# Delta rule of an RWKV-7 layer: products of k and v moved to the off-diagonal quarters of TensorE

## The chip, the cores and the metric

The kernel runs on one core of one Trainium2 chip. Its time is the device time of one launch in microseconds (us), the median of several runs. PE is TensorE, PEld its weight loads, DVE VectorE, ACT ScalarE, POOL GpSimd, SP the engine that issues the DMAs.

## The reference, cut to what matters

The whole kernel is one inference step of a two-layer decoder: an RWKV-7 layer, then a sliding-window attention layer, for a prompt of 1024 tokens and eight samples of 8 tokens. The change touches only the recurrence of the first layer. For each of 16 heads of 64 channels:

```
def step(S, inp):
    r_t, w_t, k_t, v_t, kk_t, b_t = inp
    sa = einsum('bhvk,bhk->bhv', S, kk_t)
    S = S * w_t[:, :, None, :] - sa[..., None] * b_t[:, :, None, :] + v_t[..., None] * k_t[:, :, None, :]
    return S, einsum('bhvk,bhk->bhv', S, r_t)
S_fin, ys = lax.scan(step, wkv0, seq)
```

followed by a norm of each head's output, a bonus term from r, k and v, and a multiplication by a gate. All of it is float32.

## The kernel before, in words

The stages follow one another on the core: `mixed_projections` (the projections of the first layer), `delta_rule` (the recurrence), an output projection with layer norm, the projections of the attention layer, the attention, and a last output projection. `delta_rule` begins near 491 us of the profiled span and ends near 861 us.

`delta_rule` replaces the scan by chunks of 64 tokens: 16 chunks of the prompt (`SAMPLE` is 16) and a 17th, which holds all samples. Heads stand in pairs: channels 0 to 63 of the 128 partitions are one head, 64 to 127 the other, and `DT` = 8 pairs make the 16 heads. Every product of a head is 64 by 64 (or 64 by 32, 64 by 128), with operands in one half of the partitions and its result in the same half of a PSUM bank. `HALVES` are the two halves; `for p in HALVES` issues a product of the first head and one of the second. In the 128x128 array of TensorE the first stands in the upper left quarter, the second in the lower right one. The profile writes such a product as `64*64`. Each float32 product gives two records of matmul and two of weight load.

For a chunk c these steps follow one another:

- `make_grams` (L1056): all products of b and k with kk and r over the chunk's tokens; half k = 0 of `bk` is b, k = 1 is k. `mask_grams` on DVE (L1373) cuts them to the lower triangle into `grams`. Index 0 and 1 are products of b, 2 and 3 of k.
- Inversion of the triangular matrix of index 0: POOL takes its 8x8 diagonal blocks (`small`), DVE sums them (`sum_blocks`), POOL spreads them (`pick`), PE spreads them again over the partitions (`spread_blocks`, L1089), DVE solves them by 14 small dependent instructions (`solve_blocks`, L1389), and then three levels of doubling follow: PE `make_lm` (L1097), ACT `keep_lm`, PE `grow` (L1108), DVE `add_grown` (L1413).
- `turn_rows` (L1075): b and k turned and scaled, ACT `keep_rows` into `rows`.
- `make_z` (L1119): state times kk plus grams 2 times v. `make_u` (L1139): inverse times z. `make_s` (L1148): rows of b times u plus rows of k times v. `make_y` (L1157): state times r, grams 1 times u, grams 3 times v.
- Norm, bonus and gate of y on DVE, ACT and POOL, with a transpose on PE in between (`turn_y`, L1175). DVE `gate_y` (L1464) is its end.

The order of the work is written by hand: each engine has one loop `for i in TURNS` (PE from L1218, ACT L1334, DVE L1478, POOL L1003, SP L930). In turn i chunk i + 1 is `front` (grams, rows, blocks), chunk i is inverted and gets its z, and chunk i - 1 is `behind` (u, s, y, norm). On PE a turn is: turn_y(i - 2), spread_blocks(i), make_u(behind), two quarters of the grams, make_s, make_y, the other two quarters of the grams among the levels of the inversion, turn_rows, make_z(i), the last level. Semaphores count how far each step is; an engine waits in its own order, and everything behind a waiting instruction waits too. SP issues per turn b and k, kk and r, v, the gate, and the store of y.

Two PSUM banks hold grams and then the turned rows, one z, u and s (`chain_bank`), one y (`wide_bank`), two the left factors of the inversion, two the grown parts.

Of the kernel before, what the change touches and what calls it, by code (L numbers as in the profile page):

```python
# [763 lines left out]

def first_of_delta(nc, group, a, scr):
# [20 lines left out]
    def load(sp):  # L786
# [7 lines left out]
        sp.dma_start(d["v_rows"][:, 0], scr["vt"][0]).then_inc(d["v_loaded"][0], 16)  # L794
# [8 lines left out]
def delta_rule(nc, group, a, scr, keep, outp, first, g_stored, s_stored, ahead):  # L803
# [6 lines left out]
    with Tensors(nc, "delta", group) as m:  # L810
# [22 lines left out]
        own_turned = m.sb("own_turned", 128, DT, 2, 64)  # L833
        gram_mask, level_mask, same_block, block_mask, row_pick, unit8, block_ones, ident, unit64, gn_g, gn_b, seq_mask = (
# [8 lines left out]
        consts_loaded, kr_loaded, bk_loaded, v_loaded = (first[x] for x in ("consts_loaded", "kr_loaded", "bk_loaded", "v_loaded"))  # L843
        zeroed, gate_loaded = m.sem("zeroed"), [m.sem(f"gate_loaded{k}") for k in range(2)]
        y_stored, s_loaded, kr_own_loaded = [m.sem(f"y_stored{k}") for k in range(2)], first["s_loaded"], first["kr_own_loaded"]
        state_stored = m.sem("state_stored")
        gram_made, gram_kept, small_made, coeff_made, picked, spread = (m.sem(x) for x in (
            "gram_made", "gram_kept", "small_made", "coeff_made", "picked", "spread"))
# [3 lines left out]
        end_spread, rows_made, rows_kept = m.sem("end_spread"), m.sem("rows_made"), m.sem("rows_kept")  # L852
        z_made, z_kept, u_made, u_kept, s_made, s_kept, s_ended = (m.sem(x) for x in (
            "z_made", "z_kept", "u_made", "u_kept", "s_made", "s_kept", "s_ended"))
        bonus_made, y_made, normed, y_squared, y_rooted, y_turned, y_gated = (m.sem(x) for x in (
# [5 lines left out]
        HALVES = (slice(0, 64), slice(64, 128))  # L861
        SAMPLE = 2 * TILES
# [35 lines left out]
        with nc.Block() as block:  # L898
            @block.sync
            def _(sp):  # L900
                def load_operands(c):
                    t, cols = place(c)
                    if c >= 2:
                        sp.wait_ge(rows_made, 2 * (c - 1))
# [5 lines left out]
                def load_values(c):  # L910
                    if c >= 3:
                        sp.wait_ge(y_made, c - 2)
                        sp.wait_ge(bonus_made, 2 * (c - 2))
                    sp.dma_start(v_rows[:, c % 3], scr["vt"][c]).then_inc(v_loaded[c % 3], 16)
# [15 lines left out]
                for i in range(SAMPLE + 3):  # L930
# [6 lines left out]
                    if live(i):  # L937
                        load_gate(i)
                    if i == SAMPLE + 1:

# [19 lines left out]
            def _(pool):  # L960
# [5 lines left out]
                def spread_end(c):  # L966

                    if c:
                        pool.wait_ge(rows_made, 2 * c)
# [3 lines left out]
                def scale_sample():  # L973
                    pool.wait_ge(bk_loaded[SAMPLE % 2], 16 * (SAMPLE // 2 + 1))
                    pool.wait_ge(rows_made, 2 * SAMPLE)
# [5 lines left out]
                def add_bonus(c):  # L981
                    pool.wait_ge(v_loaded[c % 3], 16 * (c // 3 + 1))
# [3 lines left out]
                    pool.tensor_tensor(bonus[:], v_rows[:, c % 3], per_head(keep["bonus"][:, c, :]), ALU.mult).then_inc(bonus_made, 1)  # L986
# [14 lines left out]

                for i in TURNS:
# [5 lines left out]
                    if 0 <= behind < SAMPLE:  # L1008
                        end_state(behind)
                    if live(behind):  # L1010
                        add_bonus(behind)
                    if live(behind) and not live(front):
                        scale_gain(behind)
                    if live(front):
                        lower = grams[:, front % 3, :, 0, :]
                        pool.wait_ge(gram_kept, 4 * front + 4)
                        if 0 <= i < SAMPLE:

                            pool.wait_ge(inv_turned, TURNED * i + 4)
                        if front:  # L1020
                            pool.wait_ge(coeff_made, front)
                        pool.tensor_tensor(small[:], lower, over_heads(same_block[:]), ALU.mult).then_inc(small_made, 1)
                        if live(behind):
                            scale_gain(behind)
                        pool.wait_ge(coeff_made, front + 1)
                        if front:
                            pool.wait_ge(spread, front)
# [1652 lines left out]
```

## Time and profile before

| | us |
|---|---|
| median of three runs | 1472.77 |
| lowest and highest run | 1472.65, 1475.62 |
| span of the profiled execution | 1471.6 |
| PE busy in it | 1411.4 (96%) |
| DVE busy in it | 794.4 (54%) |
| ACT busy in it | 575.6 (39%) |
| POOL busy in it | 249.8 (17%) |

The profiled execution is one of its own. Its page gives the span alone; the runs' times also hold what lies around it, and their lowest is 1.05 us above the span. Busy shares are over the whole kernel; the stage of the change has its own, shown further down. A row of the timeline gives the start, the length, the engine and line, output and inputs, the shape and the number of merged records; in brackets is the idle time of the engine before it and what ended it. Matmuls overlap, so the time that a group costs is read from its start to the next group's start.

### The profile page before, as it was taken

The page shows a single profiled execution, that of the slowest core. Times are in us where ns is not written, and L with a number is a line of the kernel's source. Part 1 is how long each engine was busy: PE and PEld are TensorE (multiplying, and loading weights), DVE is VectorE, ACT ScalarE, POOL GpSimd, SP SyncE. Part 2 cuts the span into 40 slices and gives each one's busy share as a digit, 9 for nine tenths or more (in the row PEclk, how much of TensorE's full clock was granted, in tenths as well). Part 3 has the DMA queues.
Part 4 walks back from the last instruction along what each step waited for, and adds up shares of the span by engine and source line. Part 5 has one row for each costly group of instructions (what it writes and reads, how often), then busy time and mean ns, then how long its engine had stood idle before and what let it go on. Part 6 is the DMA issues. An engine that isn't in the chain of part 4 may idle for free. (4 is left out here: it accounts for less than half of the span.)

```text
span 1471.6 us, 37545 instructions
## 1 busy us (share of the span) xinstructions
PE 1411.4 (96%) x16154; PEld 1281.0 (87%) x16154; DVE 794.4 (54%) x1588; ACT 575.6 (39%) x1178; POOL 249.8 (17%) x351
## 2 busy tenths in 40 slices
PE   7999999999999899999999979999999999998997
PEld 7989899887899899999999858899999997665885
DVE  6737345777831377777777753651112122775545
ACT  6726246777832022222122232441111132886324
POOL 0000000000000256555554700000001000214000
PEclk9999999999999999999999999999999998999999
DMA  5723222567596244335534255024234236431202
GB/s 207 225 60 89 74 89 90 143 188 233 167 256 179 75 97 100 74 87 118 118 88 105 68 196 186 29 111 130 88 90 119 73 108 184 137 105 33 88 29 94
DMA packets 246358, 174.00 MB, mean 118 GB/s; under 512 B 150799, under 2 KB 220367, under 8 KB 245279
## 3 DMA queue, kind: packets, MB, share of 16 engines
q1 hardware_dynamic: 214231, 156.64, 36.9%
q10 hardware_dynamic: 31968, 15.04, 3.6%
q8 instruction: 123, 2.02, 0.6%
q14 instruction: 36, 0.29, 0.1%
HBM read 111.49 MB, written 60.46 MB: 117 GB/s over the span
## 5 line engine op out<-in xcount | busy, mean ns | idle before, releaser
L369 PE MATMUL mix_acc<-mix_high,mix_w_high 128*128 128x364 f32 (+1 forms) x768 | 178.2, 341 | 11.2 <-ACT mix_high L435 9.9
L369 PE MATMUL mix_acc<-mix_low,mix_w_high 128*128 128x364 f32 (+1 forms) x768 | 172.1, 333 | 0.6 <-DVE mix_low L589 0.6
L369 PE MATMUL mix_acc<-mix_high,mix_w_low 128*128 128x364 f32 (+1 forms) x768 | 171.1, 331 | 0.0
L369 PEld LDWEIGHTS mix_acc<-mix_high,mix_w_high 128*128 128x128 f32 x768 | 130.4, 190 | 30.1 <-issue 28.3
L369 PEld LDWEIGHTS mix_acc<-mix_low,mix_w_high 128*128 128x128 f32 x768 | 133.4, 190 | 1.2 <-DVE mix_low L589 0.9
L369 PEld LDWEIGHTS mix_acc<-mix_high,mix_w_low 128*128 128x128 f32 x768 | 133.9, 190 | 0.0
L1528 PE MATMUL out_acc<-qkvg_room_r_high,qkvg_room_w_high 128*128 128x364 f32 (+1 forms) x320 | 105.8, 331 | 2.2 <-DVE qkvg_room_w_low L1880 2.2
L603 DVE TENSOR_TENSOR mix_w_low<-mix_wt,mix_w_high 128x1024 fp32r<-128x1024 f32 x32 | 39.2, 1224 | 126.1 <-ACT mix_w_high L441 125.8
L1528 PE MATMUL out_acc<-qkvg_room_r_low,qkvg_room_w_high 128*128 128x364 f32 (+1 forms) x320 | 105.1, 329 | 0.0
L1528 PE MATMUL out_acc<-qkvg_room_r_high,qkvg_room_w_low 128*128 128x364 f32 (+1 forms) x320 | 105.1, 329 | 0.0
L1878 DVE CAST qkvg_room_w_high<-qkvg_room_wt 128x1024 fp32r<-128x1024 f32 x20 | 14.0, 699 | 156.9 <-DMA qkvg_room_wt<-in_w_att 156.9
L1311 ACT ACTIVATE delta_lm<-delta_lm 128x128 f32<-128x128 f32 x96 | 24.7, 272 | 186.3 <-PE delta_lm L1105 186.3
L455 ACT ACTIVATE mix_out<-mix_acc 128x364 f32<-128x364 f32 (+1 forms) x96 | 38.3, 472 | 146.4 <-PE mix_acc L369 146.3
L1070 PE MATMUL delta_gram<-delta_kr,delta_bk 64*64 64x128 f32 x1088 | 70.8, 273 | 5.2 <-PEq L60 2.3
L584 DVE SCALAR_TENSOR_TENSOR early_xs<-early_xpad,mix_rest_mu,early_xs 128x1024 f32<-128x1024 f32 x96 | 68.7, 780 | 6.7 <-ACT early_xs L419 6.5
L288 POOL MEMSET mix_decay<- 128x16 f32 x8 | 1.0, 129 | 404.0 <-ACT mix_decay L509 404.0
L1925 ACT ACTIVATE qkvg_room_out<-out_acc 128x364 f32<-128x364 f32 (+1 forms) x40 | 18.7, 474 | 123.2 <-PE out_acc L1528 122.0
L1380 DVE TENSOR_TENSOR delta_grams<-delta_gram,delta_gram_mask 128x512 f32<-128x512 f32 x68 | 44.8, 677 | 40.8 <-PE delta_gram L1070 40.6
L1070 PEld LDWEIGHTS delta_gram<-delta_kr,delta_bk 64*64 64x64 f32 x1088 | 60.4, 135 | 6.3 <-issue 4.7
L1528 PEld LDWEIGHTS out_acc<-qkvg_room_r_high,qkvg_room_w_high 128*128 128x128 f32 x320 | 60.2, 188 | 2.5 <-issue 2.5
L2367 ACT ACTIVATE att_score<-att_score,att_low 128x256 f32<-128x256 f32 (+1 forms) x128 | 61.5, 488 | 1.5 <-DVE att_low L2404 1.5
L1713 ACT ACTIVATE begun_work<-all_x 128x1024 f32<-128x1024 f32 x18 | 19.1, 1061 | 108.4 <-DVE all_x L1778 108.4
(280 smaller groups left out, 3412.6 us busy)
## 6 DMA issues: line engine op xcount, KB each, us to landing
mix_wt<-in_w_in SPq DMA_DIRECT2D x32, 512.0 KB, 4.6
qkvg_room_wt<-in_w_att SPq DMA_DIRECT2D x20, 512.0 KB, 3.8
delta_bk<-scr_bk SPq DMA_DIRECT2D x17, 512.0 KB, 4.7
delta_kr<-scr_kr SPq DMA_DIRECT2D x17, 512.0 KB, 7.2
scr_kr<-mix_outs SPq DMA_DIRECT2D x16, 512.0 KB, 3.9
scr_bk<-mix_outs SPq DMA_DIRECT2D x16, 512.0 KB, 4.6
early_xpad<-in_xpad SPq DMA_DIRECT2D x8, 548.5 KB, 8.5
scr_xg<-early_xs SPq DMA_DIRECT2D x8, 544.0 KB, 3.0
```

The costliest lines, as they stand in the source:

```text
L369: mm = pe.matmul(acc[:, s, k, 0:width], w[:, s, d, :], r[:, d, n0:n0 + width], start=d == 0 and q == 0, stop=d == DT - 1 and q == 2)
L455: act.activation(out[:, s, n0:n0 + width], acc[:, s, k, 0:width], ACT.Silu if n >= G_ * DT else ACT.Copy).then_inc(evacuated, 1)
L584: dve.scalar_tensor_tensor(o[k], x[k], rest_mu[:, place, d:d + 1], o[k], ALU.mult, ALU.add).then_inc(mixed, 1)
L603: dve.tensor_tensor(w_low[:, n % 2], wt[:, n % 2], w_high[:, n % 2].bitcast(F32), ALU.subtract).then_inc(w_split, 1)
L1070: mm = pe.matmul(gram_bank[n % 2][p, 256 * j + 128 * k:256 * j + 128 * k + 128], bk[p, c % 2, k, pair, :], kr[p, c % 4, :, pair, :], start ...
L1311: act.activation(blocks(lm[:, lev, 4 * g:4 * g + 4, :].rearrange("p j n -> p (j n)"), lev, 0), lm_bank[g][:, 0:128].rearrange("p (m b) -> ...
L1380: dve.tensor_tensor(grams[:, c % 3, 2 * n:2 * n + 2], gram_bank[n % 2][:, :].rearrange("p (j k n) -> p j k n", j=2, k=4), mask, ALU.mult). ...
L1528: mm = pe.matmul(out, w[:, d, :], r[:, d, columns], start=d == 0 and k == 0, stop=d == DT - 1 and k == 2)
L1713: act.activation(work[:, 1], x[:, t, :], ACT.Copy, accum_out=sums[:, t:t + 1]).then_inc(summed, 1)
L1878: dve.tensor_copy(w_high[:, s], wt[:, s]).then_inc(w_rounded, 1)
L1925: act.activation(out[:, s, n0:n0 + n], banks[s][k][:, 0:n], ACT.Silu if name == "ag" else ACT.Copy).then_inc(evacuated, 1)
L2367: act.activation(score[:, t % 2, h, 0:width(t)], score[:, t % 2, h, 0:width(t)], ACT.Exp, bias=low[:, h:h + 1], accum_out=sums[:, t % 2, h ...
```

## The change

1. v is loaded with its two halves swapped (two DMAs of half the size; `v_rows`), so that the first head's v stands in partitions 64 to 127. A second, unswapped copy (`v_plain`, one more DMA of 256 KB per chunk) serves the bonus on POOL. The products of k in `make_grams` and `turn_rows` write to the other half than they read. So all products of k and v stand in the lower left or upper right quarter, those of b, u, the state and the inversion in the other two.
2. The order on PE puts each off-diagonal product beside a diagonal one of another bank: k beside b in the grams and the rows, grams 2 times v beside the last `make_lm`, grams 3 times v beside `make_u`, rows of k times v beside the end of y.
3. The grams come in two halves of four pairs instead of four quarters of two; each half fills both banks. DVE masks them in four instructions as before, of another cut.
4. `turn_y` and `gate_y` of `behind` stand at the end of a turn, not at the start of the next; `spread_blocks(front)` and the first four of seven columns of the solving too. ACT sets up the solving and POOL scales the state earlier. The mask of the third level of the inversion is dropped: `make_lm` reads `grams` there.

```
+    for half in (slice(0, 64), slice(64, 128)):
+        sp.dma_start(d["v_rows"][half, 0], scr["vt"][0, other_half(half)])...
+    FLIPPED = HALVES[::-1]
...
     def load_values(c):
         if c >= 3:
             sp.wait_ge(y_made, c - 2)
-            sp.wait_ge(bonus_made, 2 * (c - 2))
-        sp.dma_start(v_rows[:, c % 3], scr["vt"][c]).then_inc(v_loaded[c % 3], 16)
+            sp.wait_ge(s_made, c - 2)
+        for p, f in zip(HALVES, FLIPPED):
+            sp.dma_start(v_rows[f, c % 3], scr["vt"][c, p]).then_inc(v_loaded[c % 3], 16)
+    def load_plain_values(c): ...   # after load_gate(c), into v_plain
...
-    def make_grams(c, n):
+    def make_grams(c, h):
+        for j in range(4):
+            pair = 4 * h + j
+            for p in HALVES:
+                first = pe.matmul(gram_bank[0][p, 128 * j:128 * j + 128], bk[p, c % 2, 0, pair, :], kr[p, c % 4, :, pair, :], ...)
+            for p, f in zip(HALVES, FLIPPED):
+                second = pe.matmul(gram_bank[1][f, 128 * j:128 * j + 128], bk[p, c % 2, 1, pair, :], kr[p, c % 4, :, pair, :], ...)
...
+    def turn_rows(c):
+        for pair in range(DT):
+            for k, sides in enumerate((HALVES, FLIPPED)):
+                for p, f in zip(HALVES, sides):
+                    unit = end_diag[p, pair, :] if c < SAMPLE else unit64[p, :]
+                    mm = pe.matmul(gram_bank[k][f, 64 * pair:64 * pair + 64], bk[p, slot, k, pair, :], unit, ...)
...
+    def value_product(c, pair, bank, stands, begun):
+        for p, f in zip(HALVES, FLIPPED):
+            mm = pe.matmul(bank[p, 64 * pair:64 * pair + 64], stands[f], v_rows[f, c % 3, pair, :], start=pair == 0, stop=False, ...)
+        if pair == DT - 1:
+            mm.then_inc(begun, 1)
...
     # make_lm(i, 2): after each pair begin_z(i, pair) = value_product(.. chain_bank, grams 2)
     # make_u(behind): after each pair value_product(.. wide_bank, grams 3)
+    def state_of_y(c): ...          # state times r, 16 products
+    def end_y(c): ...               # grams 1 times u, after each pair value_product(.. chain_bank, rows of k)
+    def end_s(c): ...               # rows of b times u, 16 products
...
 PE, turn i:
+    make_u(behind); make_grams(front, 0); state_of_y(behind); end_y(behind)
+    make_lm(i, 0); end_s(behind); grow(i, 0); make_grams(front, 1)
+    make_lm(i, 1); grow(i, 1); turn_rows(front)
+    make_lm(i, 2, with begin_z); grow(i, 2); end_z(i)
+    turn_y(behind); spread_blocks(front)
 ACT, turn i:
+    keep_z, keep_u(behind); keep_lm(i, 0); square_y(behind); keep_lm(i, 1); begin_solving(front)
+    root(behind); keep_rows(front, 1); keep_rows(front, 0); keep_lm(i, 2)
 DVE, turn i:
+    solve_columns(i, range(4, 7)); widen_blocks(i); mask_grams(front, 0, 0); mask_grams(front, 0, 1)
+    centre_y(behind); add_grown(i, 0); mask_grams(front, 1, 0); add_state(behind); sum_squares(behind)
+    mask_grams(front, 1, 1); invert_root(behind); add_grown(i, 1); sum_blocks(front); scale_y(behind)
+    add_grown(i, 2); gate_y(behind); solve_columns(front, range(4))
 POOL, turn i:
+    spread_end(front); add_bonus(behind); sum_diagonal(front); end_state(i); scale_gain(behind)
+    pick_rows(front); mask_level(front, 0); mask_level(front, 1)
```

## Rows read from the trace of the kernel before

**Rows 1.** The page, span and its first part: busy us, share, instructions.
```profile
span 1471.6 us, 37545 instructions
PE 1411.4 (96%) x16154; PEld 1281.0 (87%) x16154; DVE 794.4 (54%) x1588; ACT 575.6 (39%) x1178; POOL 249.8 (17%) x351
```

**Rows 2.** Busy by stretch: PE, PEld, DVE, ACT, POOL, PEclk, DMA share, GB/s.
```profile
521.65:830.32 308.67, 301.34 (x8764) 296.93 (x8761) 234.15 (x585) 69.80 (x197) 181.83 (x176) 1.00 0.42 96
830.32:844.87 14.55, 13.28 (x311) 9.92 (x309) 9.09 (x23) 3.55 (x7) 11.12 (x11) 1.00 0.48 130
```

**Rows 3.** Timeline of PE over one turn of the delta rule.
```profile
642.26 0.66 PE L1182 MATMUL delta_gram<-delta_ident,delta_y 128*128 128x128 f32 x4
642.75 0.72 PE L1094 MATMUL delta_lm<-delta_pick,delta_block_ones 128*128 128x224 f32 x4
643.40 1.15 PE L1145 MATMUL delta_chain<-delta_z,delta_inv 64*64 64x64 f32 x32
644.38 1.92 PE L1070 MATMUL delta_gram<-delta_kr,delta_bk 64*64 64x128 f32 x32
646.13 0.28 PE L1154 MATMUL delta_chain<-delta_u,delta_rows 64*64 64x64 f32 x4
...
648.00 0.28 PE L1166 MATMUL delta_wide<-delta_state,delta_kr 64*64 64x64 f32 x4
...
650.80 1.04 PE L1070 MATMUL delta_gram<-delta_kr,delta_bk 64*64 64x128 f32 x16
651.67 1.07 PE L1105 MATMUL delta_lm<-delta_inv,delta_below 64*64 64x32 f32 x32
652.58 1.07 PE L1070 MATMUL delta_gram<-delta_kr,delta_bk 64*64 64x128 f32 x16
...
654.38 1.13 PE L1085 MATMUL delta_gram<-delta_end_diag,delta_bk 64*64 64x64 f32 x32
655.34 1.08 PE L1105 MATMUL delta_lm<-delta_inv,delta_below 64*64 64x32 f32 x32
...
657.78 0.31 PE L1131 MATMUL delta_chain<-delta_state,delta_kr 64*64 64x64 f32 x4
...
659.68 1.07 PE L1105 MATMUL delta_lm<-delta_inv,delta_below 64*64 64x32 f32 x32
...
662.08 0.65 PE L1182 MATMUL delta_gram<-delta_ident,delta_y 128*128 128x128 f32 x4
```

**Rows 4.** Timelines of single instants: diagonal quarters, then the attention's column and row halves.
```profile
842.07 0.27 PE L1145 MATMUL delta_chain<-delta_z,delta_inv 64*64 64x64 f32 x2 [0.56 <-ACT delta_z L1298]
...
1281.54 0.14 PEld L2330 LDWEIGHTS att_pv<-att_prob_t,att_v_rows 128*64 128x64 f32 x2 [0.33 <-issue]
...
1281.81 0.60 PE L2330 MATMUL att_pv<-att_prob_t,att_v_rows 128*64 128x256 f32 x4
...
1282.03 0.39 PE L2330 MATMUL att_pv<-att_prob_t,att_v_rows 128*64 128x256 f32 x2
...
1280.48 0.49 PE L2314 MATMUL att_sc<-att_keys,att_q_in 64*128 64x256 f32 x2
```

**Rows 5.** Timeline of DVE over the same turn.
```profile
643.56 0.21 DVE L1397 TENSOR_TENSOR delta_lm<-delta_solved,delta_lm 128x56 f32<-128x56 f32 x1
...
646.72 1.27 DVE L1407 TENSOR_TENSOR delta_inv<-delta_solved,delta_block_mask 128x512 f32<-128x512 f32 x1
...
648.73 1.25 DVE L1380 TENSOR_TENSOR delta_grams<-delta_gram,delta_gram_mask 128x512 f32<-128x512 f32 x2
...
658.61 1.04 DVE L1387 TENSOR_REDUCE delta_coeff<-delta_small 128x64 f32<-128x512 f32 x1
...
661.73 0.29 DVE L1418 TENSOR_TENSOR delta_inv<-delta_inv,delta_grown 128x128 f32<-128x128 f32 x1 [0.75 <-PE delta_grown L1115]
```

**Rows 6.** Timeline of ACT, the second copy of the turned rows.
```profile
661.29 0.60 ACT L1318 ACTIVATE delta_rows<-delta_gram 128x512 f32<-128x512 f32 x1 [0.22 <-PE delta_gram L1085]
```

**Rows 7.** What PE waited for in 520 to 845 us: total, times, longest.
```profile
PE delta_lm L1105 <- issue: 2.1, 2, 1.1
```

More of the change, by code:

```diff
@@ L762, in store_tiles, with other_half @@
     eng.dma_start(dram[TILES, :, j, 0:NB * NT], row[:, SEQ:N]).then_inc(stored, 16)
+def other_half(half):
+    return slice(64 - half.start, 128 - half.start)
 def first_of_delta(nc, group, a, scr):
@@ L1145, in make_u, with state_of_y @@
                             mm = pe.matmul(chain_bank[p, 64 * pair:64 * pair + 64], inverse(c, 1)[p, pair, :], z[p, pair, :], start=True, stop=True)
-                    mm.then_inc(u_made, 1)
-                def make_s(c):
+                        if pair == DT - 1:
+                            mm.then_inc(u_made, 1)
+                        value_product(c, pair, wide_bank, grams[:, c % 3, pair, 3, :], y_begun)
+                def state_of_y(c):
+                    pe.wait_ge(y_begun, c + 1)
+                    for pair in range(DT):
+                        for p in HALVES:
+                            o = wide_bank[p, 64 * pair:64 * pair + 64]
+                            if c < SAMPLE:
+                                pe.matmul(o, kr[p, c % 4, 1, pair, :], state[p, c % 2, pair, :], start=False, stop=False, skip_group_check=True)
+                            else:
+                                pe.matmul(o, own_turned[p, pair, 1, :], unit64[p, :], start=False, stop=False, skip_group_check=True)
@@ L1149, in make_s, with end_y @@
+                def end_y(c):
                     pe.wait_ge(u_kept, c + 1)
[L1150 removed]
+                    if c < SAMPLE:
+                        pe.wait_ge(rows_kept[1], c + 1)
                     for pair in range(DT):
[L1152 to L1154 removed]
@@ L1279, in _ @@
                     if 0 <= i < SAMPLE:
+                        wait_for_z(i)
+                        make_lm(i, 2, lambda pair: begin_z(i, pair))
                         grow(i, 2)
+                        end_z(i)
+                    if i == SAMPLE:
+                        own_values((0,))
+                        wait_for_z(i)
+                        for pair in range(DT):
+                            begin_z(i, pair)
+                        own_values((1,))
+                        end_z(i)
+                    if 0 <= behind < SAMPLE:
+                        turn_y(behind)
+                    if live(front):
+                        spread_blocks(front)
+                    if behind == SAMPLE:
+                        own_updates(range(4))
+                        own_values((4,))
+                        for pair in range(4, DT):
+                            if pair + 1 < DT:
+                                own_values((pair + 1,))
+                            own_updates((pair,))
+                        turn_y(SAMPLE)
             @block.scalar
@@ L1392, in solve_blocks @@
                     term = lm_bank[0][:, 0:64].rearrange("p (u n) -> p u n", u=8)
-                    for j in range(7):
+                    for j in columns:
                         row0 = 0 if j < 4 else 4
@@ L1521, in _ @@
                         add_grown(i, 2)
+                    if 0 <= behind < SAMPLE:
+                        gate_y(behind)
+                    if live(front):
+                        solve_columns(front, range(4))
 def three_passes(pe, out, w_high, w_low, r_high, r_low, columns):
```

309 lines of the change are left out of this document (145 added, 164 removed).

## The prediction

> **What bounds the kernel now.** I read the page first: TensorE is busy 96% of the span, DVE 54% [rows 1]. That is a mean over six stages, so I next cut out the stage that the change touches. In its 15 full turns, 521.65 to 830.32 us, PE is busy 301.3 of 308.7 us, DVE 234, POOL 182, ACT 70, and the clock is granted in full [rows 2]. Then the timeline of PE over one turn. The reader should see there that no row has a bracket with idle time: a turn takes 19.82 us, from one turn_y to the next, and is made of groups that touch [rows 3]. By starts: turn_y 0.49, spread_blocks 0.65, make_u 0.98, all grams 1.75 + 0.87 + 0.90 = 3.5, make_s 1.87, make_y 2.80, turn_rows two times 0.96, make_z 1.90, six groups of the inversion at 0.91 = 5.4. The sum is 19.5; 0.3 is lost where kinds of products change. So what is taken from PE is time won, until the next engine is full.
>
> The same rows give the price of one product. 16 products of 64 by 64 take 0.94 to 0.98 us; 16 of 32 columns take 0.91; 16 of 128 columns take 1.75 [rows 3]. So at 128 columns the streaming counts (109 ns a product), while from 64 down to 32 nothing is saved (57 to 59 ns): something else, the load of 64 weights or the issue, sets that price.
>
> **Can four quarters work at once?** All hangs on this, so I looked at single instants. After an idle stretch two matmuls of make_u are both under way within one length of 0.27 us, hence they started within 10 ns of each other: two diagonal quarters run together, and issuing takes far less than 57 ns [rows 4]. No row of this kernel has an off-diagonal quarter. Its two relations do stand in the attention. L2330 puts two products in the same 128 rows and different column halves: two weight loads of 0.13 us are both over in 0.14, four matmuls fit in 0.60 us, each streams 256 columns, and the next pair starts 0.22 us after the last (1281.81, 1282.03). Two quarters at work and two records a product make 109 ns for 128 columns also the streaming of one record, so 256 columns need 0.22 alone, so both column halves stream at once and the next loads are hidden. L2314 does the same with two row halves in the same columns, in two banks: two matmuls within 0.49 us [rows 4]. An off-diagonal quarter shares rows with one diagonal quarter and columns with the other, and the change gives it another bank; each relation by itself overlaps fully. I take it that all four do. The bounds: nothing overlaps (an off-diagonal product costs what it costs now), or all of it.
>
> The Trainium skill speaks against this. TensorE: Matmul & The Clock Gate, section The mechanism, says that a weight load overlaps with running matmuls only where the row groups differ, and an off-diagonal quarter always shares its row group with a diagonal one. By that rule the change would lose (third rival below); this trace disagrees for column halves, since the loads of L2330 cost no time between pairs in the same rows. No row here shows it for quarters.
>
> **The change on PE.** The number of products stays. Beside diagonal ones now stand: half of the grams (-1.75 us), half of turn_rows (-0.96), of make_z (-0.95), a third of make_y (-0.93) and half of make_s (-0.93). In sum -5.5, so PE needs 14.3 us a turn. DVE then becomes the bound.
>
> **The change on DVE.** It has the same instructions as before: four masks of 512 columns, 14 steps of solving, and so on; the first 8 steps are only written in the turn before, behind the same gate_y. Its busy time is 234.15 / 15 = 15.6 us a turn [rows 2]. The solving has gaps of its own: 3.16 us from first step to widening, of which 14 times 0.19 to 0.21 are busy, so 0.4 to 0.5 are gaps [rows 5]; 0.2 more elsewhere. Without any wait for others DVE needs 16.3 us.
>
> Now I walk the new order, with time 0 at the start of gate_y on DVE. DVE gates (0.6), solves (3.16), widens and transposes (2.0, from 646.72 to 648.73): the inverse is ready at 5.8. PE has begun spread_blocks at -0.2, make_u at 0.45, and goes through half the grams (0.9), state_of_y (0.95) and end_y (0.95): it is there at 4.2 and waits 1.6 for DVE. That is the first time that PE waits in a turn, and nothing is lost by it, as DVE is the bound. DVE goes on with masks, centring and the first level without more than 0.1 of waiting. The wait that DVE will have comes at the end. From the end of the second level DVE has the block sums, the scaling of y and the third level to do: 658.61 to 661.73 less the 0.75 idle is 2.4, plus 0.6, that is 3.0 [rows 5]. The other path to gate_y is: last make_lm 0.94, ACT's copy 0.5 with its latency, grow 0.91, end_z 0.95, turn_y 0.66: 4.0 [rows 3]. So DVE idles 1.0 before gate_y. ACT makes it a little worse: both copies of the rows, 0.60 each, begin 0.22 after turn_rows [rows 6] and now stand together ahead of the last copies of the inversion, which I price at 0.3. Turn: 16.3 + 1.0 + 0.3 = 17.6 us. If PE's tail were hidden it would be 16.3; if ACT's two copies were fully in the path 18.5.
>
> POOL loses one mask and has 182 / 15 = 12.1 us a turn at most [rows 2]: not a bound. It scales the state a turn earlier, which only helps add_state. The swapped v and the plain v cost SP two more issues and 256 KB more a turn at a DMA share of 0.42 [rows 2]; all are issued about a turn before their use, so nothing; without that cover, a late v would hold make_lm(2) with everything behind it on PE. spread_blocks and turn_y move by name only: they stood ahead of make_u before. New waits on PE: make_u needs y's bank free (scale_y, 1.9 us before), grams need bank 0 after gate_y (done at 0.6, needed at 1.4), end_y needs the rows of k (kept a turn earlier). Behind each stands the inversion, which would pay; each has its cover named.
>
> **Stalls.** 308.67 / 15 is 20.58, not 19.82: 11.4 us come on top, in pieces of up to 1.1 us for which the profile has only "issue" [rows 7]. They hit PE alone. With PE waiting in half of the turn, part of them falls into its waits; of 0.76 a turn I keep 0.5. New mean turn: 18.1 us (bounds 16.3 and 19).
>
> **Sum.** 15 times (20.58 - 18.1) is 37 us. Turn 0 and the two last turns have off-diagonal products too: the stretch 830.32 to 844.87 holds one more s and y (-1.9) [rows 2], turn 0 grams and rows, where DVE hides part (2 of 2.7); I take 4. 1471.6 - 41 = 1431; the profiled span stands 1.2 below the median of the runs, so 1432 us.
>
> **Rivals.**
> 1. Partial overlap. Quarters in the same rows stream together but load one after another. Then 64-column products, whose price is the load's, gain nothing, and only the grams do (two loads fit in 109 ns): PE 18.1 a turn, with the stalls 18.8, saving 15 times 1.75 and 2 more: 1444 us. For it: 32 and 64 columns cost the same now. Against: the load pair of L2330. Chance 0.10.
> 2. The change doesn't do what it says: quarters take turns in the order of issue, and PE keeps 19.8. Reordering alone frees nothing on a full PE: 1473, between 1468 and 1478. Against: all of rows 4. Chance 0.07.
> 3. Slower: products in the same rows neither stream nor load together, and the load of the second starts only when the first has streamed. A record then costs load plus stream in its row half. I take 53 ns for each: the stream is half of the 109 of 128 columns, the load no more than the 57 of the 32-column price. Four products of 64 columns, two to a row half, so four records in each: 4 times 106 = 424 ns instead of 234; four of the grams, 4 times 160 = 640 instead of 438. With 8 pairs in each of four places (rows, z, u with y, y with s) and 8 of the grams: 8 times (4 times 0.19 + 0.20) = 7.7 us a turn more, 1588 us. It decides from the point where an off-diagonal load costs more than 60 ns of standing still. Chance 0.08. This is the way of the skill's rule named above (TensorE: Matmul & The Clock Gate, The mechanism).
> The rest, 0.75, is my forecast, whose own range is 1405 (DVE without waits or stalls) to 1446 (a turn of 19, if a wait of DVE that I overlooked costs 1 us).
>
> **Range and chances.** To hold 8 in 10 I go from 1408 to 1458, which takes in rival 1. A measurement of this kernel tells about 0.2% (3 us) from no change. Faster: 0.75 + 0.10 + 0.01 = 0.86; within 0.2%: 0.05 of rival 2; slower: 0.01 + 0.08 = 0.09.
>
> **What would show it.** In the new timeline of PE: the grams of four pairs (32 records) in about 0.9 us instead of 1.75; turn_rows in 0.95 instead of 1.9; make_lm(2) with its value products in 0.95. PE idle before the first make_lm, released by DVE's transposes. DVE idle of about 1 us before gate_y, and DVE above 85% busy in the stage. Turn length 17.6 in turns without stalls. If a group with off-diagonal products takes twice as long as one without, rival 1 or 2 holds; which one, the grams tell. If DVE idles more than 2 us a turn, my walk has missed a wait.

## The result and the profile after

The changed kernel takes 1478.45 us (median of 17 runs, 1474.17 to 1487.48), the kernel before 1472.77 us (17 runs beside them, 1470.01 to 1480.83). The ratio is 1.0040, 95% interval 1.0028 to 1.0053: slower by 0.4%, where 2.8% faster was forecast. The page of the changed kernel, against [rows 1]:

```profile
span 1474.5 us, 37647 instructions
PE 1351.4 (92%) x16154; PEld 1215.1 (82%) x16154; DVE 783.9 (53%) x1588; ACT 578.9 (39%) x1178; POOL 224.0 (15%) x335
...
q8 instruction: 123, 2.02, 0.6%
```

PE is 60 us less busy and nothing is won. The last line is from the part on DMA queues: packets, MB, share. 2.02 MB in 123 packets are 16.4 KB each. PE's 16,154 pairs of weight load and matmul would be 126 packets if each packet held 128 pairs (256 instructions of 64 bytes, an estimate here). In the 15 turns after turn 0 this queue moved 69 packets, before and after alike, and PE ran 8,764 pairs, 68.5 times 128.

The stage in two windows (columns as in [rows 2]): turn 0, and the 15 turns after it.

```profile
503.05:530.31 27.26, 27.26 (x583) 26.93 (x581) 10.77 (x31) 3.76 (x11) 6.64 (x8) 0.54 0.32 71
530.31:834.68 304.37, 241.71 (x8764) 229.85 (x8761) 224.64 (x584) 73.22 (x197) 156.94 (x160) 0.97 0.50 109
```

A turn takes 304.37 / 15 = 20.29 us (before 20.58, forecast 18.1). PE idles 62.7 us in the 15 turns, 7.3 before. Turn 0 ran at half clock and took 27.26 us; before, it took 22.24 at a granted clock of 0.92.

PE's timeline in the same turn as [rows 3]:

```profile
644.17 1.16 PE L1112 MATMUL delta_gram<-delta_end_diag,delta_bk 64*64 64x64 f32 x64 [0.69 <-issue]
...
646.73 0.71 PE L1154 MATMUL delta_grown<-delta_inv,delta_lm 64*64 64x32 f32 x17 [0.45 <-ACT delta_lm L1358]
648.01 0.59 PE L1154 MATMUL delta_grown<-delta_inv,delta_lm 64*64 64x32 f32 x14 [0.58 <-issue]
...
653.95 0.32 PE L1095 MATMUL delta_gram<-delta_kr,delta_bk 64*64 64x128 f32 x1 [1.87 <-issue]
...
658.35 0.94 PE L1142 MATMUL delta_lm<-delta_inv,delta_below 64*64 64x32 f32 x25 [1.45 <-issue]
```

Two things are to be seen. `turn_rows`, 64 records at 644.17, is over at 645.13: four quarters do work at once, at 15 ns a record (before 30, [rows 3]). And the last three rows begin in the middle of groups, where no semaphore is waited for: the grow of 32 records is cut after 17, the grams after a few, a `make_lm` after 7. Between one such break and the next lie 128 matmuls (126 records in the first window; some can be missing from a trace):

```profile
648.01:653.95 5.94, 4.08 (x126) 3.69 (x125) 3.47 (x16) 1.19 (x2) 5.82 (x6) 1.00 1.14 222
653.95:658.35 4.40, 2.94 (x128) 2.83 (x128) 4.04 (x7) 0.00 (x0) 0.00 (x0) 1.00 0.52 127
```

What PE waited for in 530 to 835 us (total, times, longest), the longest groups:

```profile
PE delta_lm L1142 <- issue: 9.3, 9, 1.8
PE delta_chain L1127 <- issue: 9.0, 6, 2.1
PE delta_gram L1112 <- issue: 8.9, 15, 0.7
```

All but L1112, which comes once a turn, move from line to line as a block boundary does. Counted through from 547.41 to 698.61, the stalls marked issue stand 125 to 128 records or a multiple of that apart; only those at L1112 do not. In before the same word stood for 2.1 us at its longest group [rows 7].

L1112 is something else, although the profile writes issue there too. `turn_rows` waits for the fourth mask of DVE (L1427), and in each of the 15 turns its first matmul starts 0.10 to 0.11 us after the end of that mask. In the turn after the one above, the mask ends at 664.63 and the first matmul of L1112 starts at 664.73:

```profile
663.95 0.68 DVE L1427 TENSOR_TENSOR delta_grams<-delta_gram,delta_gram_mask 128x512 f32<-128x512 f32 x1
```

In DVE's new order this mask stands behind `add_state` and `sum_squares`. So 0.6 us a turn is a wait for DVE.

My theory after this (S): PE's instructions arrive in blocks of 128 pairs, at a rate of their own and later when loads of data fill the queues. A turn has 584 pairs, 4.56 blocks, and that sets its length. The rivals here: latencies between engines (A), and the granted clock (C).

### The profile page after: what moved, and what is told of

It is laid out like the page before. It is cut to its first block and busy times, and to the rows that moved or that the text cites. A ratio compares the mean times of both kernels' runs of the same rounds, so it can differ in the third digit from the quotient of the medians.

```text
span 1474.5 us, 37647 instructions
## 1 busy us (share of the span) xinstructions
PE 1351.4 (92%) x16154; PEld 1215.1 (82%) x16154; DVE 783.9 (53%) x1588; ACT 578.9 (39%) x1178; POOL 224.0 (15%) x335
## 3 DMA queue, kind: packets, MB, share of 16 engines
q8 instruction: 123, 2.02, 0.6%
## 5 line engine op out<-in xcount | busy, mean ns | idle before, releaser
L1154 PE MATMUL delta_grown<-delta_inv,delta_lm 64*64 64x32 f32 x1536 | 58.8, 225 | 8.9 <-issue 5.2
L1154 PEld LDWEIGHTS delta_grown<-delta_inv,delta_lm 64*64 64x64 f32 x1536 | 53.6, 141 | 11.4 <-issue 5.7
L1579 PEld LDWEIGHTS out_acc<-qkvg_room_r_low,qkvg_room_w_high 128*128 128x128 f32 x320 | 60.2, 188 | 0.0
```

The source lines that it names most:

```text
L1154: mm = pe.matmul(grown_bank[g][p, 32 * j:32 * j + 32], lm[p, lev, 4 * g + j, :], blocks(inverse(c, 1)[p, 4 * g + j, :], lev, 1), start=Tru ...
L1579: mm = pe.matmul(out, w[:, d, :], r[:, d, columns], start=d == 0 and k == 0, stop=d == DT - 1 and k == 2)
```

## Experiments

Each ratio below is to the kernel before, run beside the experiment; the changed kernel's is 1.0040. The letters of rivals in an expectation are those of its own text.

**1. Four quarters by themselves (quarters_alone).** Behind the stage, 640 products in two quarters and then 1280 in four; nobody reads them.

```
+ for n in range(40):  # HALVES into chain_bank
+ for n in range(40):  # HALVES into chain_bank, FLIPPED into wide_bank
```

> The kernel after, with products of 64 by 64 by 64 added on PE alone at the end of the delta rule, with no wait between them: first 640 in the two diagonal quarters, then 1280 in all four. Nothing is left out. Theory S (supply): PE's instructions arrive in blocks of 16 KB, 128 pairs of load and matmul, and a block takes longer to arrive than four quarters take to use it up. Then the first part (10 blocks) takes about 37 us, 29 ns a pair, and the second (20 blocks, 2560 pairs) 60 to 85 us, in bursts of 128 pairs at 14 to 15 ns with idle time between, marked issue, and one instruction packet per burst. Rival Q (quarters): four quarters never run at more than a burst's speed for a reason in the array; then idle time stands at other counts than 128. Rival W (waits of other engines): nothing waits here, so the second part takes 37 us without idle time.

Windows of the two-quarter stretch and of three blocks in four quarters:

```profile
861.83:899.37 37.54, 37.54 (x1291) 37.41 (x1291) 5.35 (x9) 1.28 (x3) 0.00 (x0) 1.00 0.11 32
...
902.85:906.60 3.75, 2.09 (x128) 1.95 (x129) 0.00 (x0) 0.00 (x0) 0.00 (x0) 1.00 0.02 4
906.60:910.63 4.03, 2.09 (x129) 1.96 (x130) 0.00 (x0) 0.00 (x0) 0.00 (x0) 1.00 0.02 4
910.63:914.38 3.75, 3.16 (x128) 2.97 (x129) 0.00 (x0) 0.00 (x0) 0.00 (x0) 0.59 0.02 4
```

Two quarters: 29 ns a pair without a gap. Four: 128 pairs in 1.87 us (14.6 ns each), then nothing until the next block; 18 blocks from 902.85 to 969.39 give 3.70 us each with the DMA queues at 2%, and in this window the instruction queue moved 18 packets and nothing else moved. In the third block the granted clock falls to 0.59, the burst takes longer, and the block still takes 3.75: the period is not the array's. This is one run, 1577.40 us with the added products. 4.56 blocks of 3.70 make 16.9 us a turn at best; before's 19.8 hid that. The Trainium skill (Runtime: NRT & Kernel Launch, Instruction fetch mechanics) describes these blocks of 16 KiB, 256 instructions, and calls the cost of a block boundary mostly hidden, because issue is slower than the refill. Here the measurement decides: 7.3 ns an instruction in the burst, 14.4 ns on average.

**2. The new order without flipping (after_diagonal).** `FLIPPED = HALVES`, and v loaded unswapped; the result is the same.

> The kernel after with its order, banks and instruction counts, but v not swapped and FLIPPED equal to HALVES: all products stand in the two diagonal quarters. Nothing is left out. S: the array needs 19.8 us a turn again and PE eats its instructions slower, so the supply hides better: turns of 20.5 to 21.5 us against 20.3 in the kernel after, the time 1478 to 1500. Rival W (the new order's waits set the turn, PE's work comes on top): the 5.5 us come back in full, turns of about 25, 1550. If the order itself was worth something, turns under 20.3.

1481.74 us, ratio 1.0063 (1.0034 to 1.0091). Turns of 312.00 / 15 = 20.80 us, PE busy in 302.55 of 312.00. Turn 0 took 19.97 at full clock, 7.3 less than with flipping. So flipping gives 15 times 0.51 = 7.6 us in the turns and loses 7.3 in turn 0; the 3 us between the medians lie outside these 16 turns. The turns did not go to 25 us, so the waits of the new order do not come on top of PE's work; before's turns are 20.58, so the order by itself is worth nothing.

**3. Fewer bytes (after_few_bytes, before_few_bytes).** From chunk 4 on the loads of b, k, kk, r, v and the gate bring one pair of eight; the products work on stale data.

```
- sp.dma_start(bk[:, c % 2], ...)
+ few = DT if c < 4 else 1
+ sp.dma_start(bk[:, c % 2, :, 0:few], ...)   # kr, v, gate likewise
```

> The kernel after with the loads of b, k, kk, r, v and the gate cut to one of eight pairs from the fifth chunk on; the old data stay, so the outputs are not the reference's. The DMA share of the stage falls from 0.5 to about 0.15, all engines do the same work. S, with the instruction fetch queued behind data: stalls marked issue shrink to under 0.5 us each and a turn falls from 20.3 towards my forecast of 17.6. S, with a fetch time of its own: turns stay within 0.5 us of 20.3. Rival W: 20.3.

> The kernel before with the same cut of its loads (outputs are not the reference's). S, fetch behind data: its stalls (0.76 us a turn) go, turns of 19.82 throughout, 1460 us. S with a fetch time of its own or W: turns as before, 20.6 on average.

The 15 turns of each, the changed kernel first:

```profile
529.81:810.41 280.60, 237.92 (x8764) 225.05 (x8761) 223.85 (x584) 73.99 (x197) 156.88 (x161) 0.99 0.19 45
```

```profile
524.84:822.36 297.52, 297.52 (x8765) 294.98 (x8761) 235.11 (x585) 69.92 (x197) 180.17 (x175) 1.00 0.18 40
```

1452.05 us (ratio 0.9858, 0.9828 to 0.9889) with turns of 18.71, and 1464.99 us (0.9944, 0.9922 to 0.9967) with turns of 19.83 and no idle time of PE at all. The 0.76 us a turn that I had put down to "stalls" before are late blocks, and the changed kernel pays 1.6 us for them (with the little that the clock adds, 0.97 against 0.99). Its turn stays well above the 16.9 us of blocks in quiet: of the 2.8 us that PE still idles in it, 0.6 is the wait of `turn_rows` and 0.6 others for DVE and ACT. So the supply is not the only thing left.

**4. More records in the kernel before (before_more_records).** 32 products of 32 columns a turn, in off-diagonal quarters beside the first level of the inversion; nobody reads them. The first `make_lm` also waits for `add_state` here, as these products write to `chain_bank`.

> The kernel before, with 32 more products of 32 columns in each of the 15 full turns (64 more pairs of weight load and matmul, issued beside the diagonal products of the first level of the inversion, into off-diagonal quarters that nobody reads). Theory S (PE's instructions come in blocks of 128 pairs and no faster than one block in 3.7 us, later when data transfers are under way; a turn of before has 584 pairs, 4.56 blocks): 648 pairs are 5.06 blocks, a floor of 18.7 us in quiet and about 22.3 us at the 4.4 us a block that the changed kernel showed; so a turn gets 1 to 2 us longer (21.5 to 22.5 instead of 20.6) although the array has room, and stretches marked issue stand 128 pairs apart. Rival A (only the array and the engines behind it count; off-diagonal products run beside the diagonal ones): turns stay at 20.6, time within 3 us of before. Rival B (each added product costs its 57 ns on the array): 32 times 57 ns is 1.8 us a turn, with no stretches marked issue between, PE busy in full.

```profile
524.62:855.20 330.58, 307.31 (x9724) 299.43 (x9721) 232.84 (x585) 71.93 (x197) 180.44 (x175) 1.00 0.41 90
```

A turn takes 22.04 us, 1.46 more. PE's busy time grew by only 6.0 us in all (0.4 a turn, against the 1.8 that 57 ns a product would cost), its idle time from 7.3 to 23.3. The stalls stand 126 to 128 records or a multiple of that apart here too. 1500.63 us, one run. S holds; an array that sets the time (A, turns of 20.6) and a price of 57 ns for each product (B) fall.

**5. Layout of the loads (after_early_packed, before_packed).** The DRAM copies of b, k, v, r and the gate stand chunk by chunk, rows of 2 and 4 KB. The first of the two also has the change of after_early_states (experiment 6).

> As the run before, and the DRAM copies of b, k, v, r and the gate are laid out chunk by chunk, so that the loads of a turn have rows of 2 and 4 KB a partition instead of 256 bytes; bytes are the same, stores on the way are cut in the same way. Theory S: these transfers take less of the queues' time (DMA share of the stage 0.50 goes to 0.3 or less), the blocks of PE's instructions come earlier, and turns go from 20.3 towards the 18.7 us of the version with an eighth of the bytes: 19.0 to 19.8; time 1455 to 1465. Rival 1: blocks are delayed by bytes and not by descriptors: turns stay at 20.2, 1470. Rival 2: the scratch stores of the projections get dearer and cost it back.

> The kernel before with the same chunk-wise layout of b, k, v, r and the gate. Theory S: its 0.76 us a turn of late instruction blocks go, as in the version with an eighth of the bytes (turns 19.83): 15 times 0.5 to 0.75 is 8 to 11 us less, about 1463. Rival 1 (bytes, not descriptors): 1472. The distance between this and the changed kernel of the same layout is what the overlap of quarters is worth when transfers disturb less: by Theory S at most 4.56 blocks of 3.7 us = 16.9 against 19.8 us a turn.

1486.23 us (ratio 1.0079, 1.0054 to 1.0104) and 1496.81 us (1.0156, 1.0136 to 1.0175), as both rivals say. The DMA share fell (0.50 to 0.37, 0.42 to 0.31), the turns stayed or grew (20.30; 20.93 against 20.58), and turn 0 began 12 to 15 us later, behind stores that took longer.

**6. Idle time of turn -1 (after_early_states, after_filled).** First two jobs of `turn_states`, then four products of 128 by 128 by 512 that nobody reads, in the places where PE waited 1.53 and 1.42 us for DVE's masks.

> The changed kernel, but in turn -1 alone the state parts of the first two jobs stand between the halves of the grams instead of behind them, so that PE has work while it waits for DVE's masks (1.53 and 1.42 us idle there, after which the granted clock is 0.50 up to about 528 us and turn 0 takes 27.3 instead of 22.2 us). Theory C (these two idle stretches bring the half clock): the clock stays full into turn 0, turn 0 takes 20 to 22 us, and the time is 5 to 9 us under the changed kernel's: 1470 to 1473. Rival: the half clock comes from somewhere else (the PE idle stretches of turn 0 itself, or the stretches before 494 us): no change, 1478. The turns after turn 0 stay at 20.3 by both.

> The changed kernel with four products of 128 by 128 by 512 that nobody reads in turn -1, two in each of the places where PE waited for DVE's masks (1.53 and 1.42 us idle). Theory C (these idle stretches let the granted clock fall to 0.50 from 494 to 528 us): the clock stays at 1.00, turn 0 takes 20 to 22 us instead of 27.3, and the time falls by 5 to 8 us to about 1471. Rival: the clock falls because of the 2.25 us of idle time at the seam of the stages, or of turn 0's own waits: then it falls all the same and the time stays within 2 us of 1478.

1476.26 us (ratio 1.0018, 0.9995 to 1.0040) and 1480.27 us (1.0043, 1.0021 to 1.0066): beside the changed kernel's 1.0040 the first may have gained 3 us, which the intervals leave open, and the second nothing. Turn 0 took 25.5 and 24.0 us instead of 27.3, with a clock of 0.59 and 0.72, but the 15 turns of the second took 20.58 us at a clock of 0.94. The two waits were not the whole cause: the narrow products of 16 columns behind them still ran at half clock. That the clock of turn 0 is no property of the code alone shows in before_few_bytes, whose turns -1 and 0 have the instructions and loads of before: its turn 0 took 24.04 us at 0.79, where before's took 22.24 at 0.92.

**7. Fewer instructions for the same result (after_merged_rows, after_merged_grams, after_merged_filled).** Two products with the same moving data become one of 128 weight columns: first in `turn_rows`, then in the grams too. b and k of the second head swap places for it, and POOL has three operations more.

```
- for k, sides in enumerate((HALVES, FLIPPED)):
-     for p, f in zip(HALVES, sides):
-         mm = pe.matmul(gram_bank[k][f, ...], bk[p, slot, k, pair, :], unit, ...)
+ for side, p in enumerate(HALVES):
+     mm = pe.matmul(gram_bank[side][:, ...], bk_pairs[p, slot, pair, :], unit, ...)
```

> The changed kernel with the two products of turn_rows that share moving data (the b and kk rows of one head, times the same end factors) made one product of 64 rows and 128 columns of weights; the result is the same. 16 products fewer a turn, that is 32 pairs of load and matmul: 552 instead of 584. Array time is the same (0.95 us a turn) if 64 by 128 products of the two row halves run side by side. Theory S (PE's instructions arrive in blocks of 128 pairs, here one in about 4.4 us, and set the turn): a quarter of a block less, so a turn goes from 20.3 to 19.2 us and the time from 1478 to about 1462. Rival A (the turn is set by latencies between PE, ACT and DVE, or by the array): turns stay at 20.3, time within 4 us of the changed kernel's. Rival B (64 by 128 products go one after another): turn_rows takes 1.9 us, turns 20.3 or longer.

> As the run before, and the two products of the grams that share moving data are made one as well; the results stand by heads in two slots, which costs POOL three operations more a turn (each over half of the partitions), and DVE's fourth mask stands ahead of add_state. 32 products fewer a turn, that is 64 pairs: 520. Theory S: half a block less, 2.2 us: turns of about 18.1 us, the time about 1446, and stretches marked issue still 128 pairs apart. From 17.6 on DVE's walk would be the bound, so less is not to be had. Rival A (latencies): the new order and POOL's longer path can only cost: turns of 20.3 to 21, time 1478 to 1490. Rival C (both): POOL's path becomes late and gives half of it back, 1460.

> Both products merged and the four fillers of turn -1 together. Theories S and C together: turns of about 18.1 us and turn 0 at full clock: 1446 less 5 to 8, about 1440. If C falls: as the merged kernel without fillers, about 1446. If S falls: 1471 to 1480.

1502.22 us (ratio 1.0177, 1.0143 to 1.0211), 1487.65 (1.0073, 1.0046 to 1.0101) and 1483.49 (1.0044, 1.0014 to 1.0075). By the times and by the mean turns (21.36, 21.37 and 20.51 us) the expectations failed. The turns with a full clock are nearer to S. Turns at a granted clock of 1.00 have a mean of 19.8 us in the changed kernel (10 of 15), 19.0 with merged rows, 18.4 to 18.6 with both (expected 19.2 and 18.1). But the others ran at 0.67 to 0.93. Two things weaken this reading. A turn with a long stall often lost the clock and so is not among these, which makes their means short. And with the merged grams the fourth mask stands ahead of `add_state`, so the wait of `turn_rows` is gone as well; how much of the step from 19.0 to 18.5 is due to it was not measured. Windows of the last kernel: a good turn, a bad one, and inside the bad one 2 us of no work and the clock after it:

```profile
608.27:626.27 18.00, 16.70 (x523) 15.76 (x521) 15.02 (x39) 4.95 (x14) 15.20 (x14) 1.00 0.54 122
663.05:687.84 24.79, 22.54 (x523) 21.60 (x521) 15.39 (x39) 4.92 (x14) 18.19 (x17) 0.72 0.45 100
668.00:670.00 2.00, 0.00 (x0) 0.00 (x0) 1.77 (x3) 0.00 (x0) 2.00 (x3) 1.00 1.08 234
...
672.00:674.00 2.00, 2.00 (x44) 2.00 (x42) 0.37 (x2) 0.56 (x1) 0.04 (x1) 0.50 0.18 44
```

What ended that idle stretch, in its timeline:

```profile
670.20 0.21 PE L1225 MATMUL delta_wide<-delta_u,delta_grams 64*64 64x64 f32 x1 [2.25 <-issue]
```

So this late block went with two costs: 2.25 us at once, and a clock of 0.50 behind it. The rows also show that merging costs time on the array, as rival B of the first expectation had it (this is `turn_rows`, 1.93 us for 32 records until the next group at 639.98, where four quarters took 0.96 for 64):

```profile
638.05 2.00 PE L1125 MATMUL delta_gram<-delta_end_diag,delta_bk 64*128 64x64 f32 x32
```

**8. The burst of loads taken apart (before_paced, after_paced, after_merged_paced).** SP issued all loads of a turn in one go, 8 to 9 us at a DMA share above 1, then nothing for 10. Now they wait for events of the turn.

```
 sp.dma_start(bk...)
+store_gated(c - 4)
+sp.wait_ge(u_made, c - 2)      # then kr
+sp.wait_ge(y_made, i)          # then v
+sp.wait_ge(s_made, i)          # then the gate and v plain
```

> The kernel before, with the loads of a turn taken apart: b and kk as soon as turn_rows frees them, then the store of the gated y, k and r only after make_u of the turn, v after y, the gate after s; the same bytes and the same instructions of PE. Theory S (blocks of PE's instructions are late when they meet the burst of loads, 8 to 9 us at a DMA share above 1): no second of the turn has such a burst, the 0.76 us a turn of stretches marked issue go mostly: turns of 19.9 to 20.2, time 6 to 10 us less than before, about 1466. Rival (lateness comes from bytes on average, not from the burst): turns stay at 20.6, 1473.

> The changed kernel with the same pacing of the loads (v plain beside the gate). Theory S: blocks at 3.7 to 4.0 us instead of 4.4: 4.56 of them are 16.9 to 18.2 us; as the version with an eighth of the bytes had turns of 18.7, I expect 18.7 to 19.3 and a time of 1453 to 1463. Rival: turns stay at 20.3, 1478.

> The merged products with the four fillers of turn -1, and the loads paced. Without pacing its turns were 17.97 us where nothing came late, but 4 of 15 ran at a granted clock of 0.67 to 0.74 and took 24.8 to 26.5, right after a stretch of 2.2 us marked issue. Theory C2 (such late blocks are what lets the clock fall): with fewer of them all turns take 18.0 to 18.5, the clock stays above 0.97 in the stage, and the time is about 1440 to 1450. Rival (the clock falls by itself because PE has too little to do in a turn): turns of 25 us stay, 1475 to 1490.

before_paced: 1469.04 us, ratio 0.9961 (0.9945 to 0.9977), turns 301.45 / 15 = 20.10. after_paced: 1474.40, 1.0005 (0.9990 to 1.0020); PE idles 54.5 us instead of 62.7, and a turn at full clock takes 19.5 us instead of 19.8 (5 turns against 10, which themselves spread from 18.6 to 21.0), but the clock's mean is 0.94 and the mean turn 20.32. after_merged_paced: 1473.82, 0.9979 (0.9952 to 1.0005), runs from 1460.63 to 1490.72; its trace, of the 1490.72 us, has five turns at 0.67 to 0.72. Pacing helped the kernel before by 0.5 us a turn, as S says; in the changed kernel its gain is not clear of the spread, and the lower clock stands against it.

**9. One filler a turn (after_merged_paced_filled, after_turn_filled, after_all).** A product of 128 by 128 by 384 that nobody reads, where PE waits for DVE ahead of the first `make_lm`.

```
+ pe.matmul(grown_bank[1][:, 128:512], block_ones[:], kr[:, i % 4, 0, 0:6]..., start=True, stop=True)
  make_lm(i, 0)
```

> As the run before, and in each turn one product of 128 by 128 by 384 that nobody reads (about 0.6 us, one more product and two pairs a turn) where PE waits 0.8 us for DVE before the first make_lm. If PE's idle time lets the clock fall: fewer turns at a lower clock than in the run before, time the same or up to 10 us less, 1438 to 1445. If only the late blocks do: the same as the run before within 3 us.

> The changed kernel with nothing but one product of 128 by 128 by 384 a turn that nobody reads, in front of the first make_lm, where PE waits for DVE. Theory C2 (PE's idle time lets the granted clock fall, here to a mean of 0.97 over the 15 turns): the clock stays at 1.00, which gives back what the five turns at 0.87 to 0.92 cost, some 5 us; supply of 586 pairs at 4.4 us a block stays, so turns of 19.8 to 20.3 and a time of 1472 to 1478. If the clock is all that holds the changed kernel back: turns of 18, 1445. If the filler only costs its 0.66 us a turn: 1485.

> Merged products, paced loads and the filler of every turn (1462 us), and six more fillers of 128 by 128 by 384 around the narrow products of the sample's states in turns -1 and 0, where the granted clock was 0.50 from 506 to 536 us and turn 0 took 30.9 us. Theory C2: the clock stays at 1.00, turn 0 takes 21 to 24 us with the fillers, the time falls by 5 to 9 us to 1453 to 1458. If the clock falls at the seam of the stages whatever PE does after it: the time rises by the fillers' 4 us at most, 1462 to 1466.

after_merged_paced_filled: 1462.32 us, ratio 0.9920 (0.9901 to 0.9939), 11.5 us under the median of the run before, though not at the 1438 to 1445 expected; turns of 18.70 us, all 15 at 1.00:

```profile
537.16:817.73 280.57, 266.44 (x7835) 242.95 (x7831) 228.40 (x584) 76.13 (x197) 217.56 (x202) 1.00 0.48 118
```

The two traces compared here are unlike: that of the unfilled kernel is the longest of its twelve runs, and its two shortest, 1460.63 and 1461.25 us, are as short as the filled kernel's six (1461.4 to 1463.73). What the filler did was to take away the long runs; that one product a turn is the cause rests on these six and twelve runs.

after_turn_filled: 1484.52 us, 1.0089 (1.0062 to 1.0117), mean clock 0.96, turns 20.62. In the kernel with 586 pairs a turn the late blocks stay, and by S their idle stretches can't be filled (there is no instruction to fill them with). The regular wait at this place is also nearly absent: PE waited for DVE ahead of `make_lm` in 2 of the changed kernel's 15 turns, 1.4 us in all. The filler only costs. after_all, with six fillers more in turns -1 and 0: 1458.04 us, 0.9895 (0.9871 to 0.9920). Turn 0 took 25.39 us at 0.80 instead of 30.86 at 0.52. This version beats both kernels, by 1.0 and 1.4%.

## Why the prediction was wrong

**What held.** Four quarters work at once: half the grams 0.90 us, `turn_rows` 0.96, `make_lm(2)` with its value products 0.95, as written down beforehand. Rivals 1 to 3 fall, the third with the Trainium skill's rule (TensorE: Matmul & The Clock Gate, The mechanism): loads in the same rows cost no wait. That the time came out near rival 2's (1468 to 1478) is chance: its mechanism, quarters that take turns, did not occur. DVE's busy time was 15.0 us a turn (15.6 taken), PE's at full clock 15.7 (14.3 taken), and neither was the bound.

**What failed: "PE needs 14.3 us a turn. DVE then becomes the bound".** I summed array times and took the supply of instructions to be free. It has a price: 3.70 us for 128 pairs in quiet, and beside the loads 4.40 and 5.94 in the two blocks quoted above, and 4.36 on the mean of experiment 4 (22.04 us for 5.06 blocks, an estimate that puts the whole turn down to them). 4.56 times 4.36 is 19.9 us, and the full-clock turns of the changed kernel take 19.8. The change halves the time of a record and keeps their number. The hint stood in the profile before: a queue called "instruction", and stalls of up to 1.1 us for which it had only "issue" [rows 7].

**"Of 0.76 a turn I keep 0.5".** I supposed that PE's new waits would swallow the stalls. They grew: PE idled 4.2 us a turn, 0.6 of it at L1112 and about 3.2 in the other stretches marked issue. A faster PE meets the next block earlier; it does not wait less for it.

**The walk.** It had one wait of PE in a turn, before the first `make_lm`, for the inverse. That one came in 2 turns of 15. It missed the wait of `turn_rows` for DVE's fourth mask, 0.6 us in every turn. Its own signs said so: DVE was to be over 85% busy and was at 74% (224.64 of 304.37 us), and an idle time of DVE over 2 us was to mean a missed wait; it was 5.3.

**The clock.** The sum had none, since the stage before ran at 1.00 [rows 2]. A PE with idle stretches lost it: in the changed kernel five turns were at 0.87 to 0.98 and took 21.2 us against 19.8, with the same 4.2 us of idle time, which is 7 us by the clock; turn 0 at 0.54 cost 5.0 more than before instead of saving 2; with turn -1 the stage was 8.7 us late at turn 1. In after_diagonal, where PE idled 0.6 us a turn, the clock stood at 1.00 in turn 0 and in all 15 after it. That the idle time is the cause is argued from such pairs; the fillers of experiments 6 and 9 brought the clock back only in part or only in the merged kernel.

**The sum, in the profiled executions.** Forecast -41, measured +2.9 (1471.6 to 1474.5). The 15 turns gave 4.3 instead of 37.2: 33 missing, 7 by the clock and 26 in turns at full clock. In those 26 the late blocks are the main part by their idle time (3.2 us a turn against the 0.5 kept) and the wait of `turn_rows` (0.6) the lesser one; what each adds to a turn was not taken apart. Up to turn 1 it was 8.7 late instead of 2 ahead: 10.7. The last two turns and the rest gave 1.5 where 1.9 was hoped. The rival for the other side should have been this one; mine, loads that don't overlap, was contradicted by rows in hand.

What stays open: which bytes delay a block (the packed layout had a lower DMA share and no faster blocks, the eighth of the bytes had), what moving the fourth mask alone would give the changed kernel, what lets the clock fall in turn 0, and why full-clock turns of the merged kernels still vary from 18.0 to 20.1 us.

## What to carry to other kernels

Before you price a change that makes many small products faster, count PE's instructions in a turn: in these runs 128 pairs of load and matmul came every 3.7 us on average, and every 4.4 or so where loads ran beside them. Below about 29 ns a pair an array that works faster only waited longer; fewer, larger instructions then shortened the turns at full clock even where they took more array time, but the kernel's time only once the clock was held too. An idle stretch marked issue is not always late supply: count the records between such stretches, and look for a semaphore that the line waits for. And an idle stretch of PE is not free even off the critical path: look at the granted clock turn by turn. Filling a regular wait gained 11 us in the merged kernel; in the changed kernel, whose idle time stood elsewhere, it cost time (1.0089 against 1.0040).

## What the runs showed of the hardware

- Four 64 by 64 quarters of float32 run side by side: 128 pairs in 1.87 us, two quarters 3.7 (29 ns a pair).
- The supply of PE's instructions: 3.70 us per 128 pairs on the mean of 18 blocks at a DMA share of 0.02, with one packet of the instruction queue for each; 3.75 in the block with a granted clock of 0.59; 4.40 and 5.94 in two blocks beside loads (DMA share 0.52 and 1.14).
- After 2.25 us without work PE's granted clock went from 1.00 to 0.50 (1.2 of 2.4 GHz) within 2 us and stayed there for 13 us, with PE busy throughout; a turn then took 24.8 us instead of 18.0. With one product of 0.6 us a turn, in a wait of 0.8, it stood at 1.00 in all 15 turns; without it 5 of 15 turns were at 0.67 to 0.72 in the longest of twelve runs.
- 64 by 128 products in two row halves take 60 ns a record at 64 columns of moving data, against 15 for 64 by 64 in four quarters.
